# Attention and conv projections of an encoder layer: the high weights meet high and low tokens in one product of 512 columns

## What is computed

```python
proj = x @ w_in                                # conv input, q, k, v, branch gates
gates = sigmoid(proj[..., G_OFF:] + b_gate)
g_conv, g_attn = gates[..., :D_MODEL], gates[..., D_MODEL:]
conv_out = conformer_conv(conv_u, ...)         # ... layer norm, silu, then @ w_conv_proj
attn_out = windowed_gqa(q, k, v, ...) @ w_attn_proj
mixed = (g_conv * conv_out + g_attn * attn_out) @ w_out
x = layer_norm(ALPHA * x + mixed)
x = layer_norm(ALPHA * x + hierarchical_moe(x))   # 32 experts, top 2 of one group
```

## Time and profile before

| | |
|---|---|
| median of 3 runs | 473.58 us (473.19 to 473.99) |
| the profiled execution | 473.26 us; span from first to last instruction 471.5 us |
| mean granted TensorE clock | 0.994 of full speed |
| TensorE busy | 463.3 us (98%), 2788 products |
| VectorE, ScalarE, GpSimd busy | 244.2, 208.9, 223.2 us |
| DMA | 145.14 MB, mean 308 GB/s |

### The profile page before, as it was taken

The page is one execution under the profiler, slowest core; times in us unless marked ns, Lnnn a source line. Parts: engine busy times, 40 slices in busy tenths (PEclk is TensorE's granted clock), DMA queues, the critical chain, the costliest instruction groups (busy, mean ns, idle before and its releaser), DMA issues.

```text
span 471.5 us, 7554 instructions
## 1 busy us (share of the span) xinstructions
PE 463.3 (98%) x2788; PEld 323.0 (69%) x2788; DVE 244.2 (52%) x543; ACT 208.9 (44%) x467; POOL 223.2 (47%) x190
## 2 busy tenths in 40 slices
PE   8999999999999999999999999999999999999994
PEld 7999999989999999998873544444444334444431
DVE  3089899868998566356377532222222222222115
ACT  4544555478975679454683422221211122222213
POOL 3998899946866578999546121111111001111002
PEclk9999999999999999999999999999999999999997
DMA  8899989634443345899947989999999999999922
GB/s 292 291 378 360 343 301 359 198 120 140 164 133 135 136 134 177 295 358 341 340 187 281 423 325 419 422 423 420 422 420 422 421 422 420 420 420 423 423 116 91
DMA packets 27093, 145.14 MB, mean 308 GB/s; under 512 B 3120, under 2 KB 3376, under 8 KB 14512
## 3 DMA queue, kind: packets, MB, share of 16 engines
q1 hardware_dynamic: 27056, 144.65, 78.9%
HBM read 143.59 MB, written 1.05 MB: 307 GB/s over the span
## 4 chain that ended last, share of the span: by engine, by line
PE 94%; ACT 3%; DVE 1%; issue 1%; POOL 0%; ACTq 0%; DVEq 0%; POOLq 0%
PE bank L1638 23%; PE bank L1379 14%; PE bank L1381 13%; PE bank L1380 13%; PE bank L1676 12%; PE bank L1699 4%; PE bank L1700 3%; PE bank L1459 1%; PE bank L1437 1%; PE bank L1407 1%; PE bank L1664 1%; DVE stat L1136 1%; PE bank L1613 1%; PE bank L1612 1%; PE bank L1447 1%
## 5 line engine op out<-in xcount | busy, mean ns | idle before, releaser
L576 POOL TENSOR_TENSOR w_lo<-raw,w_hi 128x512 fp32r<-128x512 f32 x140 | 182.8, 1324 | 44.0 <-ACT w_hi L647 41.0
L647 ACT CAST w_hi<-raw 128x512 fp32r<-128x512 f32 x140 | 85.3, 620 | 77.3 <-PE bank L1381 71.2
L1379 PE MATMUL bank<-x_hi,w_hi 128*128 128x256 f32 x400 | 115.5, 289 | 0.1
L1381 PE MATMUL bank<-x_hi,w_lo 128*128 128x256 f32 x400 | 113.1, 283 | 0.0
L1380 PE MATMUL bank<-x_lo,w_hi 128*128 128x256 f32 x400 | 113.1, 283 | 0.0
L932 DVE SCALAR_TENSOR_TENSOR bank<-slots,par,bank 128x256 f32<-128x256 f32 x232 | 92.3, 480 | 0.3
L605 POOL COPY raw<-gates 128x512 f32 x28 | 19.8, 709 | 144.7 <-PE bank L1638 133.5
L1638 PE MATMUL bank<-slots,raw 128*64 128x512 f32 x352 | 77.7, 593 | 0.0
L1379 PEld LDWEIGHTS bank<-x_hi,w_hi 128*128 128x128 f32 x400 | 76.6, 192 | 0.8 <-POOL w_lo L576 0.5
L1380 PEld LDWEIGHTS bank<-x_lo,w_hi 128*128 128x128 f32 x400 | 76.7, 192 | 0.3
L1381 PEld LDWEIGHTS bank<-x_hi,w_lo 128*128 128x128 f32 x400 | 76.7, 192 | 0.0
(11 more groups left out here) (234 smaller groups left out, 653.2 us busy)
## 6 DMA issues: line engine op xcount, KB each, us to landing
slots<-in_w_gate_up SPq DMA_DIRECT2D x44, 1024.0 KB, 12.5
raw<-in_w_in SPq DMA_DIRECT2D x45, 512.0 KB, 4.3
slots<-in_w_down SPq DMA_DIRECT2D x20, 1024.0 KB, 13.2
extra<-in_w_gate_up SPq DMA_DIRECT2D x10, 1024.0 KB, 13.4
spare<-in_w_gate_up SPq DMA_DIRECT2D x10, 1024.0 KB, 15.6
late<-in_w_down SPq DMA_DIRECT2D x10, 1024.0 KB, 16.2
raw<-in_w_attn SPq DMA_DIRECT2D x8, 512.0 KB, 3.3
raw<-in_w_conv SPq DMA_DIRECT2D x8, 512.0 KB, 3.8
```

Of the source, the lines that this page charges most:

```text
L576: nc.gpsimd.tensor_tensor(w_lo[:, n % SPLIT, m], raw[:, raw_of(b), m], w_hi[:, n % SPLIT, m].bitcast(F32), ALU.subtract).then_inc(w_lo_don ...
L647: nc.scalar.copy(w_hi[:, n % SPLIT, m], raw[:, raw_of(b), m]).then_inc(w_hi_done, 1)
L1379: mm(dst, ah, bh, start=first, stop=False, **kw)
L1381: return mm(dst, al, bh, start=False, stop=last, **kw)
```

## The change

In the attention and conv projections TensorE now multiplies the high weights by the high and the low tokens in one product of 512 columns, which fills a whole PSUM bank: high by high in its first 256 columns, high by low in the others. The product of low weights and high tokens goes on into the first 256 columns. For this `x_hi` and `x_lo`, and `a_hi` and `a_lo`, become the halves of one tensor each. Every block now takes a bank of its own (`wide_bank`), and TensorE may start pair q when pair q-2 has been read. ScalarE copies the second half of each of a pair's two banks to SBUF (`second_part`, in the space of `pT`), VectorE adds the first halves, and the gates are multiplied by the sum in SBUF. The two products behind `written` move from before block 56 to before block 58, with a wait for the last attention pair's gating. The output projection keeps its three products.

```diff
@@ -187,9 +187,11 @@
         wr_sb = sb("wr", [P, KT * LOGITS + HALF_ROWS // 2])
         wr = wr_sb[:, 0:KT * LOGITS].rearrange("p (k n) -> p k n", k=KT)
         x_at = nc.sbuf_base
-        x_hi, x_lo = sb("x_hi", [P, KT, SEQ], F32R), sb("x_lo", [P, KT, SEQ], F32R)
+        x_both = sb("x_both", [P, 2, KT, SEQ], F32R)
+        x_hi, x_lo = x_both[:, 0, :, :], x_both[:, 1, :, :]
         a_at = nc.sbuf_base
-        a_hi, a_lo = sb("a_hi", [P, KT, SEQ], F32R), sb("a_lo", [P, KT, SEQ], F32R)
+        a_both = sb("a_both", [P, 2, KT, SEQ], F32R)
+        a_hi, a_lo = a_both[:, 0, :, :], a_both[:, 1, :, :]
         w_hi = sb("w_hi", [P, SPLIT, D], F32R)
         w_lo_at = nc.sbuf_base
         w_lo = sb("w_lo", [P, SPLIT, D], F32R)
@@ -242,8 +244,8 @@
         x1T = raw[:, 0:2, :].rearrange("p a (b t) -> p (a b) t", t=SEQ)
 
 
-        x1_hi = x_hi[:].rearrange("p i t -> p (i t)").rearrange("p (t n) -> p t n", t=TT)
-        x1_lo = x_lo[:].rearrange("p i t -> p (i t)").rearrange("p (t n) -> p t n", t=TT)
+        x1_hi = x_hi.rearrange("p i t -> p (i t)").rearrange("p (t n) -> p t n", t=TT)
+        x1_lo = x_lo.rearrange("p i t -> p (i t)").rearrange("p (t n) -> p t n", t=TT)
         compact = w_hi[:, 1, :].rearrange("p (t n) -> p t n", t=TT)
         xgT = gates[:].rearrange("p a t -> p (a t)").rearrange("p (k n) -> p k n", k=KT)
         y_hi, y_lo = w_hi[:, 0, :], w_lo[:, 0, :]
@@ -345,6 +347,7 @@
         prob_ready, p_turned, p_copied = sem("prob_ready"), sem("p_turned"), sem("p_copied")
         pv_done, o_hi_done, o_lo_done = sem("pv_done"), sem("o_hi_done"), sem("o_lo_done")
         attn_gated, conv_gated, merged = sem("attn_gated"), sem("conv_gated"), sem("merged")
+        part_copied = sem("part_copied")
         m_hi_done, m_lo_done = sem("m_hi_done"), sem("m_lo_done")
         mean_done, centered, squared, var_done = (sem(n) for n in ("mean_done", "centered", "squared", "var_done"))
         summed, squares_summed = sem("summed"), sem("squares_summed")
@@ -424,6 +427,17 @@
 
             return (b - len(NATIVE)) // RAW + (2 if raw_of(b) == 0 else 1)
 
+        def wide_bank(b):
+
+            q = b // 2
+            if q % 2 == 0:
+                return bank[b % 2]
+            return bank[2] if b % 2 == 0 else bank[6 if b < B_CONV else 7]
+
+        def second_part(q):
+
+            return pT[:, q % 2, :, :]
+
         def wait_pair_read(eng, q):
 
             if q < Q_BLOCK // 2:
@@ -671,7 +685,13 @@
                         ins = nc.scalar.activation(gates[:, c, :], src[:, j * SEQ:(j + 1) * SEQ], ACT.Sigmoid,
                                                    bias=par[:, A_BGATE + c:A_BGATE + c + 1])
                     ins.then_inc(gates_done, 1)
-                elif q >= B_CONV // 2:
+                elif q >= B_ATTN // 2:
+                    if q >= B_ATTN // 2 + 2:
+                        wait_pair_read(act, q - 2)
+                    for j in range(2):
+                        ins = nc.scalar.copy(second_part(q)[:, j, :], wide_bank(2 * q + j)[:, SEQ:])
+                    ins.then_inc(part_copied, 1)
+                if q >= B_CONV // 2:
                     m = q - B_CONV // 2
                     act.wait_ge(merged, m + 1)
                     nc.scalar.copy(a_hi[:, 2 * m:2 * m + 2, :], gates[:, 2 * m:2 * m + 2, :]).then_inc(m_hi_done, 1)
@@ -991,6 +1011,14 @@
                                             rstd_bank[:, 0:SEQ].unsqueeze(1).broadcast_to([P, 2, SEQ]),
                                             ALU.mult).then_inc(scaled, 1)
 
+            def add_parts(q):
+
+                dve.wait_ge(part_copied, q - B_ATTN // 2 + 1)
+                for j in range(2):
+                    part = second_part(q)[:, j, :]
+                    ins = nc.vector.tensor_tensor(part, wide_bank(2 * q + j)[:, 0:SEQ], part, ALU.add)
+                chained(ins)
+
             def evacuate(q):
                 src = pair_bank[q % PSUM_PAIRS]
                 if q < Q_BLOCK // 2:
@@ -1002,15 +1030,15 @@
                     m = q - N_IN // 2
                     dve.wait_ge(block_done, 2 * q + 2)
                     dve.wait_ge(gates_done, N_IN // 2 - GATE_BLOCK // 2)
+                    add_parts(q)
                     g = gates[:, KT + 2 * m:KT + 2 * m + 2, :]
-                    nc.vector.tensor_tensor(g, src[:].rearrange("p (a t) -> p a t", a=2), g,
-                                            ALU.mult).then_inc(attn_gated, 1)
+                    nc.vector.tensor_tensor(g, second_part(q), g, ALU.mult).then_inc(attn_gated, 1)
                 elif q >= B_CONV // 2:
                     m = q - B_CONV // 2
                     g, other = gates[:, 2 * m:2 * m + 2, :], gates[:, KT + 2 * m:KT + 2 * m + 2, :]
                     dve.wait_ge(block_done, 2 * q + 2)
-                    nc.vector.tensor_tensor(g, src[:].rearrange("p (a t) -> p a t", a=2), g,
-                                            ALU.mult).then_inc(conv_gated, 1)
+                    add_parts(q)
+                    nc.vector.tensor_tensor(g, second_part(q), g, ALU.mult).then_inc(conv_gated, 1)
                     dve.wait_ge(conv_gated, m + 1)
                     dve.wait_ge(attn_gated, m + 1)
                     nc.vector.tensor_tensor(g, g, other, ALU.add).then_inc(merged, 1)
@@ -1399,6 +1427,28 @@
                         ins.then_inc(half_done, 1)
                 ins.then_inc(block_done, 1)
 
+            def wide_block(b, both, hi, tile_ready=None):
+
+                q = b // 2
+                dst = wide_bank(b)
+                if b < B_ATTN + 3:
+                    wait_pair_read(pe, b - 27)
+                elif b % 2 == 0:
+                    wait_pair_read(pe, q - 2)
+                n = splits_before(b)
+                for k in range(KT):
+                    if k % 4 == 0:
+                        pe.wait_ge(w_lo_done, 2 * n + k // 4 + 1)
+                    if tile_ready is not None:
+                        pe.wait_ge(tile_ready, k + 1)
+                    w = slice(k * P, (k + 1) * P)
+                    mm(dst[:].rearrange("p (a t) -> p a t", a=2), w_hi[:, n % SPLIT, w], both[:, :, k, :],
+                       start=(k == 0), stop=False)
+                    ins = mm(dst[:, 0:SEQ], w_lo[:, n % SPLIT, w], hi[:, k, :], start=False, stop=(k == KT - 1))
+                    if k == 3:
+                        ins.then_inc(half_done, 1)
+                ins.then_inc(block_done, 1)
+
             def native_blocks():
 
                 for k in range(KT):
@@ -1497,7 +1547,7 @@
                     pe.wait_ge(summed, 1)
                     average(mean_bank, mean_done, True)
             for b in range(B_ATTN, B_CONV):
-                column_block(b, a_hi, a_lo, o_lo_done if b == B_ATTN else None)
+                wide_block(b, a_both, a_hi, o_lo_done if b == B_ATTN else None)
                 if b == B_VAR:
                     pe.wait_ge(squares_summed, 1)
                     average(var_bank, var_done, False)
@@ -1508,11 +1558,13 @@
                     mm(wr_bank[:, 1, :], ones[:], wr_sums[:, 1, :], start=True, stop=True).then_inc(wr_means_done, 1)
 
             pe.wait_ge(wr_ready, 1)
-            for n in (2, 3):
-                ins = mm(out_bank[n][:], a_hi[:, 0, 0:P], a_hi[:, 0:2, :], start=True, stop=True)
-            ins.then_inc(written, 1)
             for b in range(B_CONV, B_OUT):
-                column_block(b, x_hi, x_lo, c_lo_done if b == B_CONV else None)
+                if b == B_CONV + 2:
+                    pe.wait_ge(attn_gated, KT // 2)
+                    for n in (2, 3):
+                        ins = mm(out_bank[n][:], x_hi[:, 0, 0:P], x_hi[:, 0:2, :], start=True, stop=True)
+                    ins.then_inc(written, 1)
+                wide_block(b, x_both, x_hi, c_lo_done if b == B_CONV else None)
             pe.wait_ge(residual_set, 2 * TT)
             for b in range(B_OUT, N_BLOCKS):
                 k = b - B_OUT
```

## The result

The changed kernel took 481.43 us (median of 5 runs, 481.42 to 481.75), the kernel before 473.58 (5 runs, 473.19 to 474.19). The ratio is 1.0167 with a 95% interval of 1.0156 to 1.0178: 7.85 us slower, where 481.3 was forecast.

The account below looks back on a forecast made before the run. In blocks 48 to 71 TensorE had 1.05 us of slack before the ScalarE and GpSimd weight supply bound it; delays at blocks 56 to 66 sum to 7.75 us, so 473.58 + 7.7 = 481.3 us, range 476.6 to 484.

Parts of the forecast that it names:

- 56: Attention: copies in ScalarE's full stretch delay block 56's cast and first w_lo half; TensorE starts it 1.2 us later.
- 58: Pair 27's product and the x_lo operations hold GpSimd up twice in blocks 56 and 57: 0.75 us more.
- 60: Conv pair 28: copies, additions, product and merge delay a_hi and block 60's weight cast: 0.95 us more.
- 62: Closed loop without TensorE takes 7.29 us per pair against 5.76: 1.5 us more at block 62.
- 64: The same conv loop, 7.29 us per pair against 5.76, adds another 1.5 us at block 64.
- 66: Pair 64/65 took 5.45 us before and meets the same 7.29 us cycle: 1.85 us more.
- The cycle: Conv, per pair: four GpSimd halves of 1.25, product, merge, a_hi cast and weight cast, 7.29 us in all.
- The signs that I named: TensorE waits 1 to 1.8 us at blocks 60 to 66, later merges 1.2 to 1.8, GpSimd idles a microsecond and more.
- The waits that I costed at nothing: Pair q−2's gating, residual writes needing banks 5 and 6, and SyncE's raw loads behind w_lo: no cost.
- 0.4 us margin: In the conv cycle the product asks 0.4 us too late for the port gap at 203.76.
- rival (a): Conv product gets the port one half earlier, cycle 6.04, total 477.6 us (476.2 if free of the port); chance 0.24.
- attention loss: Evacuations 24 to 26 add 1.86 us to ScalarE's full stretch before block 56, where TensorE starts 1.2 us later.

Follow-up runs that it names:

- e4: Changed kernel without ScalarE's copies and VectorE's additions, high-by-low half thrown away, gates multiplied by the first half in PSUM: 473.12 us.
- e1: Changed kernel with the sum of the two parts kept in PSUM and the gates multiplied there in two 256-column products: 478.59 us.
- e3: Changed kernel with ScalarE's wait for merged and its a_hi cast moved behind the weight casts of the next block: 477.67 us.
- e8: Kernel before with only ScalarE's wait for merged and the a_hi cast moved behind the next block's weight casts: 473.77 us.
- e2: Changed kernel with ScalarE's copies in the four conv pairs placed between the block's two weight casts, one cast earlier: 479.91 us.
- e9: Changed kernel with the sum in PSUM, so the product needs no port, and ScalarE's conv copies one cast earlier: 476.07 us.
- e10: Changed kernel with only the attention projection changed and ScalarE's copies of the second parts left out there: 474.52 us.
- e5: Changed kernel with only the attention projection changed; conv has its three 256-column products and gating of the kernel before: 475.32 us.
- e7: Changed kernel with the sum in PSUM and ScalarE's wait for merged behind the next block's casts: 475.33 us.
- e12: Only conv changed, sum in PSUM, wait for merged behind the next casts; product, merge and a_lo subtraction in PSUM too: 472.81 us.
- e6: Changed kernel with only the conv projection changed; the attention projection is that of the kernel before: 480.49 us.

## Why the prediction was right

**The sum, term by term.** From the starts of the blocks in both traces, counted from block 48, the delay grows by:

| at block | forecast | measured | before, after |
|---|---|---|---|
| 56 | +1.2 | +1.14 | 25.52, 26.66 |
| 58 | +0.75 | +0.57 | 31.25, 32.96 |
| 60 | +0.95 | +1.19 | 37.01, 39.91 |
| 62 | +1.5 | +1.50 | 42.77, 47.17 |
| 64 | +1.5 | +1.51 | 48.53, 54.44 |
| 66 | +1.85 | +1.79 | 54.00, 61.70 |

The sum is 7.70 at block 66 and 7.79 at the last product of block 71, against 7.75. That it came so near is in part luck: the forecast was 0.18 too high at block 58 and 0.24 too low at block 60. The total has luck in it too: the profiled executions differ by 481.43 − 473.26 = 8.17 = 7.79 − 0.38 (block 48 started earlier) + 0.76 in the tail (last section), and the forecast had neither of the last two. With one trace of each, it is not shown whether the change has a part in them.

**The prices.** Two copies took 0.64 from start to end (0.7 said), the two additions 0.76 (0.8), the product 1.41 with its wait, the merge 1.67. TensorE's k takes 0.347 (0.347 said), though not by the parts that I gave: the product of 512 columns takes 0.23 to 0.24 and the other 0.11 to 0.12, where 0.227 and 0.120 were said. Little of the saving arrives, as e4 shows. The cycle is 7.27 against 7.29. I counted a half of w_lo at 1.25 there and at 1.283 further up; single records start 1.25 apart. The signs that I named are there: TensorE waits 1.5 to 1.9 us at blocks 60 to 66, the merge takes 1.66 to 1.67 from pair 29 on, and GpSimd idles 1.80 in each cycle, more than the microsecond I had in mind.

**The two causes.** e1 and e3 separate them: the product at the port takes 2.6 us of the stretch, the place of ScalarE's wait 4.1, both together 6.4 (they overlap by 0.3), and what is left, 1.35, is the attention part less TensorE's saving in conv. e8 shows that the second is a cost of the change only. The waits that I costed at nothing (pair q−2, the residual, the raw ring) do not appear in the view of waits between 160 and 245 us: no product waits for a gating and no cast for a load; SyncE's loads wait for w_lo, as forecast.

**Where I was loose.** I treated the 0.4 us margin of rival (a) as a switch for all cycles. e2 and e9 show that half a microsecond wins the gap in some of them and loses it again in the next. For a product free of the port rival (a) gave a cycle of 5.55 and 476.2; e1 measured 6.84 and 478.59, since the merge missed the gap that I had given it. The statement that the attention loss is ScalarE's alone is also too simple: e10 leaves 0.76 without the copies, of which the x_lo operations' waits at the port and the new place of the two products behind `written` each have a part.

## What to carry to other kernels

Read the slack of the buffer that feeds the bound engine before pricing a saving on that engine: here 1.05 us of slack stood against 1.5 us of new work in the loop that refills it, and a saving of 1.7 us on TensorE became a loss of 7.8. Where an engine's program holds a wait ahead of work that feeds the others, look at what the change adds in front of that wait, and try to move the wait before you shorten the work (e3: 4.1 us, against 2.6 for e1). A VectorE operation with two SBUF inputs beside GpSimd's busy stream here waited for the rest of GpSimd's instruction and took its own time from GpSimd (the product: 1.41 us, against 0.76 for two halves with one input in PSUM; a half of w_lo: up to 1.74 instead of 1.29). Keep one input in PSUM where such a stream runs.

## What the runs showed of the hardware

**The port is not handed over at the last moment.** In e1 the merge asks at 210.71 and GpSimd's next half starts at 210.73, in e9 at 203.24 and 203.25: both waited for that half as well (1.87 and 1.84 us for an operation that takes 0.69 when nothing holds it up). In e9 at 216.00, with the next half starting at 216.06, the merge went first (0.69), and so did the product of e2 at 204.02 (0.69), with the half that starts at 204.11 lasting 1.75. So in these traces 0.06 us ahead was enough and 0.02 was not; GpSimd's records are rough, and these are few cases.

**A busy GpSimd starves VectorE.** The four x_lo operations took 5.83 us in e10 and 3.60 in the changed kernel; two of them took 0.75 with GpSimd idle.

**The last four products run at either clock.** TensorE waits 2.45 us for VectorE before them. The rows are of the kernel before, then of the changed one, then of e8:

```profile
464.67 2.96 PE L1761 MATMUL bank<-slots,sig 128*128 128x512 f32 x4 [2.45 <-DVE bank L1364]
```

```profile
472.07 3.65 PE L1813 MATMUL bank<-slots,sig 128*128 128x512 f32 x4 [2.45 <-DVE bank L1392]
```

```profile
465.66 1.96 PE L1764 MATMUL bank<-slots,sig 128*128 128x512 f32 x4 [2.45 <-DVE bank L1367]
```

In the changed kernel the granted clock is 0.55 and 0.50 (the 1.2 GHz level) over the first two microseconds of these products, in the kernel before 0.94 over the first and 0.50 over the second. From the last product of block 71 to the end of the span it is 239.49 us in the changed kernel, 238.73 before, 238.4 to 238.75 in e3 to e5 and e7 to e12, and 239.5 to 239.65 in e1, e2 and e6, a spread of 1.25 us. Up to the first of these four products the distance is 231.87 to 231.89 in all kernels but e6 (232.03), so the spread arises behind it, in instructions that no edit touches. Whether an edit brings it about by the time at which these products start is not shown.
